# Column sums of ten conditioning halves: folded on VectorE and spread by one matmul, in a diffusion backbone layer on one core

## The chip, the core and the metric

The kernel runs on one NeuronCore of a Trainium2 chip. The metric is the time of one execution on the device, in microseconds (us), and the median of several runs stands for a kernel. The engines go by their short names: PE is TensorE (PEld its weight loads), DVE is VectorE, ACT is ScalarE, POOL is GpSimd, and SP issues most of the DMAs. Each engine runs its own list of instructions in order, and they meet only by semaphores.

## What is computed

One layer over 256 latent tokens (x) and 256 context tokens (y) of width 2048: a half-step SwiGLU block of width 5632, a mixer (gated recurrence and long convolution) behind one input projection, a second half-step SwiGLU block for the latent tokens, and a last norm. What matters for the change are the modulation vectors. Two vectors c are put through SiLU and multiplied by one large matrix; the nine parts of 2048 columns are shifts, scales and gates.

```python
mx = [m[:, None, :] for m in jnp.split(jax.nn.silu(c) @ ada_w[l] + ada_b[l], N_MOD, axis=-1)]
mc = jnp.split(jax.nn.silu(c_ctx) @ ada_w[l] + ada_b[l], N_MOD, axis=-1)

x = x + 0.5 * mx[2] * _swiglu(_modulate(_rmsnorm(x, norm_ffn1[l]), mx[0], mx[1]), ...)
y = y + 0.5 * mc[2] * _swiglu(_modulate(_rmsnorm(y, norm_ffn1[l]), mc[0], mc[1]), ...)
hc = _modulate(_rmsnorm(y, norm_mix[l]), mc[3], mc[4])
hx = _modulate(_rmsnorm(x, norm_mix[l]), mx[3], mx[4])
x = x + mx[5] * (mix_x @ w_out[l])
x = x + 0.5 * mx[8] * _swiglu(_modulate(_rmsnorm(x, norm_ffn2[l]), mx[6], mx[7]), ...)
return _rmsnorm(x, final_norm)
```

So parts 0 to 2 are needed in the first block, and parts 3 to 8 (mixer and second block) only after it. Of parts 5 to 8 only the latent vector counts.

## The kernel before

**Units.** All large weights stream in units of 128x1024 fp32 (512 KB). SP loads a unit into one of four raw buffers (`load_unit`), ACT rounds it to w_hi (L381), DVE takes the rest w_lo = raw - w_hi (L386), three units ahead of PE (`AHEAD`), and PE multiplies. In the first block each unit is 24 matmuls of 512 columns: for each of eight 128x128 blocks the three passes L396, L397 and L398. PE works through 24 units in each chunk of the first block: units 0 to 7 (j) are the up projections of the next chunk, 8 to 15 the down projection (`down`), and 16 to 23 again up. The down projection gives 16 output blocks d, two in each unit, and goes round three PSUM banks (4, 5, 6); when a block is done, DVE adds it to the residual stream in two instructions (`add`, L843), and only then may PE take that bank for block d + 3. Bank 7 is left for the modulation sums.

**Modulation.** The matrix has 18 halves of 1024 columns, each read in 16 tiles of 128 rows. Halves 0 to 3 are done in the prologue on PE. The rest are done by DVE beside the matmuls of the first block: `ada_step` multiplies a 128x1024 tile by a column of SiLU(c) and adds it to a running total (L610 for the first tile, L613 for the others). After 16 tiles the total, 128 lanes by 1024 columns, has to be summed over its lanes. `ada_total` (L640) does that on PE: for each 128x128 block of the total one fp32 matmul with a column of ones, which puts the sums of 128 columns along the lanes of bank 7. `ada_take` (L658, for halves 4 and 5 `ada_finish`) then copies them to `mods`.

**Order.** The chunks of the first block are `F1_LOOPS = ((1, 3), (4, 2), (4, 1), (1, 0))`: one chunk with halves 4 and 5 (ada 3), four iterations with one half for both vectors each (ada 2: halves 6 to 9), four iterations with two halves for the latent vector each (ada 1: halves 10 to 17), one chunk without, and then the last down projection. Where the steps and sums stand in the 24 units is written in `ada_steps`, `ADA_SUM_AT` and `ADA_TAKE_AT`: for ada 2 the 16 steps are in units 0 to 15, the sum behind unit 18; for ada 1 the steps are in units 0 to 7 and 11 to 18, the sums behind units 10 and 21. After the last down projection PE does the norm of the context (L455), DVE adds the bias to all the parts (`finish_mods`, L1867), and the mixer begins.

## Time and profile before

| | us |
|---|---|
| median of 3 runs | 3262.28 |
| lowest, highest | 3249.78, 3262.71 |
| the profiled execution's own time | 3266.25 |
| its span, from the first to the last instruction | 3264.5 |

The profile is of one execution. A group of instructions in it has a source line of the kernel, the engine, what it writes and reads, the count, the busy time, the mean ns of one, and the time for which the engine sat idle just before them with what ended it. PE's matmuls are pipelined, so one that is shown as 0.39 us long may start every 0.23 us: what a matmul costs in a row of them is read from the distance of the starts. An fp32 matmul is recorded as two. The granted clock (PEclk) is 1.00 at TensorE's upper level (2.4 GHz) and 0.50 at its lower one (1.2 GHz); a stretch in between holds a share of each.

### The profile page before, as it was taken

To read this page: it belongs to the slowest core of one execution; us is meant where nothing else is said; L and a number is where in the kernel's file an instruction comes from. 1 tells how busy PE (TensorE), PEld (TensorE's weight loads), DVE (VectorE), ACT (ScalarE), POOL (GpSimd) and SP (SyncE) were. 2 spreads that over 40 slices of the span, in tenths; PEclk is the share of its full clock that TensorE was granted. 3 is DMA by queue.
4 is the path that set the end of the run, shared out by engine and by line. 5 is a ranking of instruction groups with operands and counts; after the bars stand their busy time and mean duration, and the time that the engine had idled before them with its cause. 6 is when DMAs were issued, how large, how long until landed. Compare 5 with 4: busy or idle time off the path is not lost. (4 is left out here: it accounts for less than half of the span.)

```text
span 3264.5 us, 46521 instructions
## 1 busy us (share of the span) xinstructions
PE 3152.6 (97%) x17388; PEld 2694.0 (83%) x17388; DVE 2136.2 (65%) x2907; ACT 1262.5 (39%) x1687; POOL 187.9 (6%) x194
## 2 busy tenths in 40 slices
PE   6889999999999999999998999999998999999997
PEld 3348788888888888888877999999997888888886
DVE  5577747558475675756447767776666667766677
ACT  5452121222212222222236777753334444444443
POOL 3300000000000000000000023330000000000000
PEclk8889899999999999999999999999999999999998
DMA  8556545535446576665324554445545565666663
GB/s 299 181 193 185 176 147 150 180 129 173 146 143 219 187 238 214 223 218 173 97 91 123 162 175 149 148 142 187 163 145 152 184 190 182 185 190 184 186 185 110
DMA packets 438914, 563.25 MB, mean 173 GB/s; under 512 B 17856, under 2 KB 395065, under 8 KB 437897
## 3 DMA queue, kind: packets, MB, share of 16 engines
q1 hardware_dynamic: 432208, 545.80, 53.6%
q0 software_dynamic: 2816, 9.43, 0.9%
q10 hardware_dynamic: 3768, 6.37, 0.5%
q8 instruction: 81, 1.33, 0.2%
q14 instruction: 41, 0.33, 0.0%
HBM read 553.14 MB, written 8.39 MB: 172 GB/s over the span
## 5 line engine op out<-in xcount | busy, mean ns | idle before, releaser
L386 DVE TENSOR_TENSOR w_lo<-raw,w_hi 128x1024 fp32r<-128x1024 f32 x736 | 909.7, 1241 | 792.2 <-ACT w_hi L381 788.8
L381 ACT ACTIVATE w_hi<-raw 128x1024 fp32r<-128x1024 f32 x736 | 774.9, 1057 | 1365.6 <-PE bank L398 1067.1
L396 PE MATMUL bank<-h_hi,w_hi 128*128 128x512 f32 x1408 | 553.2, 393 | 0.2 <-DVE w_lo L386 0.2
L397 PE MATMUL bank<-h_lo,w_hi 128*128 128x512 f32 x1408 | 551.7, 392 | 0.0
L398 PE MATMUL bank<-h_hi,w_lo 128*128 128x512 f32 x1408 | 551.6, 392 | 0.0
L402 PE MATMUL bank<-h,w_hi 128*128 128x512 f32 x1408 | 500.9, 400 | 7.1 <-DVE h L473 6.6
L403 PE MATMUL bank<-h,w_lo 128*128 128x256 f32 x1408 | 396.6, 282 | 0.0
L613 DVE SCALAR_TENSOR_TENSOR states<-ada_raw,silu_c,states 128x1024 f32<-128x1024 f32 x300 | 375.9, 1281 | 2.3
L402 PEld LDWEIGHTS bank<-h,w_hi 128*128 128x128 f32 x1408 | 266.0, 189 | 74.5 <-DVE h L473 7.3
L396 PEld LDWEIGHTS bank<-h_hi,w_hi 128*128 128x128 f32 x1408 | 266.8, 189 | 56.5 <-issue 1.0
L398 PEld LDWEIGHTS bank<-h_hi,w_lo 128*128 128x128 f32 x1408 | 266.7, 189 | 56.3
L397 PEld LDWEIGHTS bank<-h_lo,w_hi 128*128 128x128 f32 x1408 | 266.8, 189 | 55.3
L396 PE MATMUL bank<-hx_hi,w_hi 128*128 128x256 f32 x1024 | 296.1, 289 | 0.0
L398 PE MATMUL bank<-hx_hi,w_lo 128*128 128x256 f32 x1024 | 289.6, 283 | 0.0
L397 PE MATMUL bank<-hx_lo,w_hi 128*128 128x256 f32 x1024 | 289.6, 283 | 0.0
L396 PE MATMUL bank<-g_hi,w_hi 128*128 128x512 f32 x704 | 277.9, 395 | 7.6 <-DVE y_res L843 4.8
L397 PE MATMUL bank<-g_lo,w_hi 128*128 128x512 f32 x704 | 276.9, 393 | 0.0
L398 PE MATMUL bank<-g_hi,w_lo 128*128 128x512 f32 x704 | 276.4, 393 | 0.0
L403 PEld LDWEIGHTS bank<-h,w_lo 128*128 128x128 f32 x1408 | 267.4, 190 | 0.0
L402 PE MATMUL bank<-g_both,w_hi 128*128 128x512 f32 x704 | 252.0, 402 | 6.2 <-DVE x_res L850 3.3
L403 PE MATMUL bank<-g_both,w_lo 128*128 128x256 f32 x704 | 198.8, 282 | 0.0
L397 PEld LDWEIGHTS bank<-hx_lo,w_hi 128*128 128x128 f32 x1024 | 196.3, 192 | 0.5 <-issue 0.2
(269 smaller groups left out, 4301.7 us busy)
## 6 DMA issues: line engine op xcount, KB each, us to landing
raw<-in_ffn_w_dram SPq DMA_DIRECT2D x528, 512.0 KB, 3.7
ada_raw<-in_ada_w_dram SPq DMA_DIRECT2D x256, 512.0 KB, 4.5
raw<-in_w_in_dram SPq DMA_DIRECT2D x176, 512.0 KB, 3.9
raw<-in_ada_w_dram SPq DMA_DIRECT2D x32, 512.0 KB, 4.5
raw<-in_w_out_dram SPq DMA_DIRECT2D x32, 512.0 KB, 3.6
spec<-spec_spill POOLq DMA_DIRECT2D x8, 768.0 KB, 5.0
spec_spill<-spec_out ACTq DMA_DIRECT2D x4, 1280.0 KB, 6.9
xin<-in_x_dram SPq DMA_DIRECT2D x1, 2048.0 KB, 14.1
```

Source lines behind the costliest of these rows:

```text
L381: nc.scalar.activation(w_hi[un.slot(j)][:], raw[un.slot(j)][:], ACT.Copy).then_inc(hi_done, 1)
L386: nc.vector.tensor_tensor(w_lo[un.slot(j)][:], raw[un.slot(j)][:], w_hi[un.slot(j)][:].bitcast(F32), ALU.subtract).then_inc(lo_done, 1)
L396: nc.tensor.matmul(o, w_hi[slot][:, c0:c0 + P], hi, start=start, stop=False, skip_group_check=True)
L397: nc.tensor.matmul(o, w_hi[slot][:, c0:c0 + P], lo, start=False, stop=False, skip_group_check=True)
L398: return nc.tensor.matmul(o, w_lo[slot][:, c0:c0 + P], hi, start=False, stop=stop, skip_group_check=True)
L402: nc.tensor.matmul(o, w_hi[slot][:, c0:c0 + P], both, start=start, stop=False, skip_group_check=True)
L403: return nc.tensor.matmul(o[:, 0:SEQ], w_lo[slot][:, c0:c0 + P], hi, start=False, stop=stop, skip_group_check=True)
L613: nc.vector.scalar_tensor_tensor(out=total, in0=src, scalar=silu_c[:, m, t:t + 1], in1=total, op0=ALU.mult, op1=ALU.add).then_inc(done, 1)
```

## The change

The two halves 4 and 5 stay as they are. For the other twelve halves, of which four are for two vectors (16 totals in all), `ada_total` on PE and `ada_take` go. In their place:

- DVE folds each total itself (`ada_fold_lanes`): 512 columns at a time it transposes 32x32 blocks from the total into bank 7, and sums each run of 32 along the row, which leaves 16 numbers on each lane. That is two transposes and two sums for each total. The numbers go to a 128x512 tile `ada_cols` that takes the place of the small `rows` tiles. The folds stand behind units 16 and 17 in the ada 2 iterations, and behind units 8 and 19 in the ada 1 iterations (`ADA_FOLD_AT`).
- Four partial sums are still apart, one in each group of 32 lanes. One fp32 matmul of 512 columns with a 128x128 matrix of zeros and ones, `same_lane`, adds them for all tiles at once (`ada_spread`). It stands ahead of unit 2 of the last down projection of the first block.
- Twelve copies of 32 lanes on DVE (`ada_gather`), behind unit 3 of the same down projection, bring the result into `mods`.
- `same_lane` is built by four small DVE instructions in the prologue (`lanes`), behind `bounds_rest` at tile 34. The 128x128 tile of ones shrinks to one column.
- The first step of a new total no longer waits for PE (L606), except in halves 4 and 5. PE gets a wait for the gathered values ahead of the norm L455.

```diff
-        ones_1 = sb("ones_1", [P, P])
-        rows = [sb(f"rows{n}", [P, P]) for n in range(4)]
+        same_lane = sb("same_lane", [P, P])
+        rows4 = sb("rows", [P, 4, P])
+        rows = [rows4[:, n, :] for n in range(4)]
+        ada_cols = rows4[:].rearrange("p n c -> p (n c)")
...
-        ADA_SUM_AT = {3: {2: (4, 0), 11: (3, 0)}, 2: {18: (2, 0)}, 1: {10: (1, 0), 21: (1, 1)}, 0: {}}
-        ADA_TAKE_AT = {2: {19: 0}, 1: {11: 0, 22: 1}}
+        ADA_SUM_AT = {3: {2: (4, 0), 11: (3, 0)}, 2: {}, 1: {}, 0: {}}
+        ADA_FOLD_AT = {3: {}, 2: {16: 0, 17: 1}, 1: {8: 0, 19: 1}, 0: {}}
...
-            if m == 0:
-                ve.wait_ge(ada_pe, ada_half(ada, it, n) + (0 if n else 1))
+            if m == 0 and ada >= 3:
+                ve.wait_ge(ada_pe, ada_half(ada, it, n) + 1)
...
-        def ada_take(ve, half, to, streams):
-
-            ve.wait_ge(ada_pe, half + 2)
-            nc.vector.tensor_copy(mods_flat[:, bass.ds(half * 8, 8), 0:streams],
-                                  bank[to][:, 0:16].rearrange("p (b t) -> p b t", t=2)[:, :, 0:streams]).then_inc(ada_out, 1)
+        def ada_fold_lanes(ve, ada, it, n):
+
+            total, done = ada_even[n], (ada_x, ada_c)[n if ada == 2 else 0]
+            nth = ada_folded(ada, it, n)
+            ve.wait_ge(done, ada_done(ada, it, 0 if ada == 2 else n, KB))
+            for h in range(2):
+                ve.wait_ge(ada_fold, nth + (2 * h + 1))
+                nc.vector.transpose(bank[7][:], total[:, h * 512:(h + 1) * 512]).then_inc(ada_fold, 1)
+                ve.wait_ge(ada_fold, nth + (2 * h + 2))
+                nc.vector.reduce_sum(ada_cols[:, bass.ds(nth * 8 + h * 16, 16)],
+                                     bank[7][:].rearrange("p (b i) -> p b i", i=32), mybir.AxisListType.X).then_inc(ada_fold, 1)
...
+        def ada_spread(pe):
+
+            pe.wait_ge(ada_fold, FOLDED)
+            pe.wait_ge(c_split, 6)
+            nc.tensor.matmul(bank[7][:], same_lane[:], ada_cols, start=True, stop=True).then_inc(ada_pe, 1)
+
+        def ada_gather(ve):
+
+            ve.wait_ge(ada_pe, 2 + 4 + 2)
+            for q in range(4):
+                lanes = slice(32 * q, 32 * q + 32)
+                src = bank[7][lanes, :].rearrange("p (i k q) -> p i k q", k=8, q=4)[:, :, :, q]
+                for t in range(2):
+                    nc.vector.tensor_copy(mods_flat[lanes, 6 * 8:10 * 8, t].rearrange("p (a k) -> p a k", k=8),
+                                          src[:, 0:8].rearrange("p (a t) k -> p a t k", t=2)[:, :, t])
+                ins = nc.vector.tensor_copy(mods_flat[lanes, 10 * 8:18 * 8, 0].rearrange("p (a k) -> p a k", k=8), src[:, 8:16])
+            ins.then_inc(ada_out, 1)
...
             for j in range(8):
+                if j == 2 and len(loops) > 1:
+                    ada_spread(pe)
                 down(un, j, j, N_CHUNK - 1)
...
-                    if ada in (1, 2) and j in ADA_TAKE_AT[ada]:
-                        ada_take(ve, ada_half(ada, it, ADA_TAKE_AT[ada][j]), 7, ada_streams(ada))
+                    if len(loops) > 1 and j in ADA_FOLD_AT[ada]:
+                        ada_fold_lanes(ve, ada, it, ADA_FOLD_AT[ada][j])
...
+                if j == 3 and len(loops) > 1:
+                    ada_gather(ve)
...
+            pe.wait_ge(ada_out, 8)
             norm_pe(pe, nctx, 512)
...
+            def lanes():
+                nc.vector.tensor_tensor(same_lane[:, 0:64], ident[:, 0:64], ident[:, 64:128], ALU.add).then_inc(c_split, 1)
+                ve.wait_ge(c_split, 3)
+                nc.vector.tensor_tensor(same_lane[:, 0:32], same_lane[:, 0:32], same_lane[:, 32:64], ALU.add).then_inc(c_split, 1)
+                ve.wait_ge(c_split, 4)
+                nc.vector.tensor_copy(same_lane[:, 32:64], same_lane[:, 0:32]).then_inc(c_split, 1)
+                ve.wait_ge(c_split, 5)
+                nc.vector.tensor_copy(same_lane[:, 64:128], same_lane[:, 0:64]).then_inc(c_split, 1)
```

What that does to the lists of instructions is seen at two places. The first is PE in the body of the ada 1 iterations, at the end of unit 10. Before, eight fp32 matmuls on blocks of the total (`states`) stand between the third pass of one unit and the first pass of the next:

```order
L396 MATMUL bank<-g_hi,w_hi 128x512
L397 MATMUL bank<-g_lo,w_hi 128x512
L398 MATMUL bank<-g_hi,w_lo 128x512
L707 ISA
L710 REGISTER_ALU
L640 MATMUL bank<-ones,states 128x1 x8
L690 REGISTER_ALU
L695 REGISTER_ALU
L396 MATMUL bank<-g_hi,w_hi 128x512
```

In the changed kernel nothing of this is in the loop bodies of ada 2 and ada 1, and the one matmul that takes its place stands in the last down projection (lines are those of the changed kernel):

```order
L401 MATMUL bank<-g_lo,w_hi 128x512
L402 MATMUL bank<-g_hi,w_lo 128x512
L681 MATMUL bank<-rows,same_lane 128x512
L400 MATMUL bank<-g_hi,w_hi 128x512
L401 MATMUL bank<-g_lo,w_hi 128x512
```

The second place is DVE in the same body, behind unit 8. Before, the next unit's w_lo follows the two residual additions at once:

```order
L843 SCALAR_TENSOR_TENSOR x_res<-bank,gate,x_res 128x256
L843 SCALAR_TENSOR_TENSOR y_res<-bank,gate,y_res 128x256
L386 TENSOR_TENSOR w_lo<-raw,w_hi 128x1024
L838 REGISTER_ALU
L843 SCALAR_TENSOR_TENSOR x_res<-bank,gate,x_res 128x256
```

In the changed kernel the four instructions of a fold stand between them:

```order
L879 SCALAR_TENSOR_TENSOR y_res<-bank,gate,y_res 128x256
L667 REGISTER_ALU
L669 ISA
L670 STREAM_TRANSPOSE bank<-states 128x512
L671 REGISTER_ALU
L672 ISA
L672 TENSOR_REDUCE rows<-bank 128x16
L669 REGISTER_ALU
L670 STREAM_TRANSPOSE bank<-states 128x512
L671 REGISTER_ALU
L672 ISA
L672 TENSOR_REDUCE rows<-bank 128x16
```

So both the w_lo of a later unit and the residual additions of unit 9 come behind the fold.

## Rows read from the trace of the kernel before

**Rows 1.** The page: busy time, then PE's granted clock in 40 slices.
```profile
PE 3152.6 (97%) x17388; PEld 2694.0 (83%) x17388; DVE 2136.2 (65%) x2907; ACT 1262.5 (39%) x1687; POOL 187.9 (6%) x194
...
PEclk8889899999999999999999999999999999999998
```

**Rows 2.** Groups by line, 560 to 1600 us (busy, mean ns, idle before).
```profile
L396 PE MATMUL bank<-h_hi,w_hi 128*128 128x512 f32 x1007 | 395.0, 392 | 0.0
```

**Rows 3.** Groups by line, whole span.
```profile
L640 PE MATMUL bank<-ones,states 128*128 128x1 f32 x320 | 38.0, 251 | 0.0
```

**Rows 4.** Timeline of PE (start, length) round a sum of 16 matmuls.
```profile
564.67 0.39 PE L398 MATMUL bank<-h_hi,w_lo 128*128 128x512 f32 x1
564.90 3.63 PE L640 MATMUL bank<-ones,states 128*128 128x1 f32 x32
568.38 0.49 PE L396 MATMUL bank<-h_hi,w_hi 128*128 128x512 f32 x1
568.71 0.40 PE L397 MATMUL bank<-h_lo,w_hi 128*128 128x512 f32 x1
```

**Rows 5.** The same round a sum of 8 matmuls.
```profile
1064.30 0.39 PE L398 MATMUL bank<-g_hi,w_lo 128*128 128x512 f32 x1
1064.53 1.84 PE L640 MATMUL bank<-ones,states 128*128 128x1 f32 x16
1066.23 0.49 PE L396 MATMUL bank<-g_hi,w_hi 128*128 128x512 f32 x1
```

**Rows 6.** Table of windows: busy time of each engine, then PEclk, DMA share, GB/s.
```profile
703.00:707.00 4.00, 4.00 (x12) 3.10 (x11) 0.07 (x1) 0.00 (x0) 0.00 (x0) 0.57 0.41 124
838.00:846.00 8.00, 8.00 (x31) 6.51 (x31) 0.17 (x1) 0.17 (x1) 0.00 (x0) 0.79 0.21 66
970.00:982.00 12.00, 12.00 (x56) 10.55 (x55) 1.40 (x2) 1.06 (x1) 0.00 (x0) 0.72 0.23 70
1050.00:1587.00 537.00, 537.00 (x2433) 446.79 (x2432) 326.66 (x377) 118.28 (x128) 0.00 (x0) 1.00 0.63 202
1675.00:1680.00 5.00, 4.75 (x14) 3.76 (x15) 1.43 (x3) 0.36 (x1) 0.00 (x0) 0.66 0.35 105
2510.00:3200.00 690.00, 690.00 (x3907) 598.35 (x3906) 489.74 (x732) 310.30 (x412) 0.00 (x0) 1.00 0.61 186
```

**Rows 7.** Groups by line, whole span: DVE instructions of 512 columns.
```profile
L805 DVE TENSOR_TENSOR xn<-xn,bank 128x512 f32<-128x512 f32 x22 | 14.1, 684 | 32.5 <-PE bank L398 32.5
...
L1979 DVE RECIPROCAL rstd<-root 128x512 f32<-128x512 f32 x4 | 13.4, 3342 | 0.0
```

**Rows 8.** Timeline of DVE: a copy of 512 columns.
```profile
1683.41 0.42 DVE L437 COPY sq_sum<-sq 128x512 f32<-128x512 f32 x1
```

**Rows 9.** Timeline of DVE behind units 8 and 19 of an ada 1 iteration.
```profile
1054.25 0.47 DVE L843 SCALAR_TENSOR_TENSOR y_res<-bank,gate,y_res 128x256 f32<-128x256 f32 x1
1054.94 1.23 DVE L386 TENSOR_TENSOR w_lo<-raw,w_hi 128x1024 fp32r<-128x1024 f32 x1 [0.22 <-ACT w_hi L381]
...
1062.01 0.48 DVE L843 SCALAR_TENSOR_TENSOR x_res<-bank,gate,x_res 128x256 f32<-128x256 f32 x1 [0.40 <-PE bank L398]
...
1117.68 1.23 DVE L386 TENSOR_TENSOR w_lo<-raw,w_hi 128x1024 fp32r<-128x1024 f32 x1 [5.27 <-ACT w_hi L381]
```

**Rows 10.** Timeline of DVE behind units 16 and 17 of an ada 2 iteration.
```profile
689.50 1.23 DVE L386 TENSOR_TENSOR w_lo<-raw,w_hi 128x1024 fp32r<-128x1024 f32 x1 [3.09 <-ACT w_hi L381]
694.94 1.23 DVE L386 TENSOR_TENSOR w_lo<-raw,w_hi 128x1024 fp32r<-128x1024 f32 x1 [4.21 <-ACT w_hi L381]
```

**Rows 11.** Timeline of PE: its one wait at a chunk's end, and the norm L455.
```profile
1675.25 0.50 PE L396 MATMUL bank<-g_hi,w_hi 128*128 128x512 f32 x1 [2.83 <-DVE g_lo L826]
...
1723.11 1.42 PE L455 MATMUL bank<-sq_sum,ones_d 128*128 128x512 f32 x2 [2.45 <-DVE sq_sum L440]
```

**Rows 12.** Timeline of DVE in the last down projection, behind unit 3.
```profile
1701.56 1.23 DVE L386 TENSOR_TENSOR w_lo<-raw,w_hi 128x1024 fp32r<-128x1024 f32 x1 [1.14 <-ACT w_hi L381]
```

**Rows 13.** Timeline of DVE in the prologue: the instruction that follows `bounds_rest`.
```profile
121.81 0.18 DVE L1789 RECIPROCAL hy_cols<-bank 128x4 f32<-128x4 f32 x1 [2.60 <-PE bank L1174]
```

More of the change, by code:

```diff
@@ L168, in build @@
         pairs4 = sb("pairs4", [P, 64])
+        one_col = pairs4[:, 2:3]
         lb = sb("lb", [P, 2, HEADS])
@@ L298, in build @@
         ada_x = sem("ada_x")
+        ada_fold = sem("ada_fold")
         ada_c = sem("ada_c")
@@ L640, in ada_total @@
                     ins = nc.tensor.matmul(bank[to][:, 2 * b + t:2 * b + t + 1], sums[t][:, b * P:(b + 1) * P],
-                                           ones_1[:, 0:1], start=fresh and b == 0 and t == 0, stop=True,
+                                           one_col, start=fresh and b == 0 and t == 0, stop=True,
                                            skip_group_check=True)
@@ L653, in ada_finish, with ada_folded @@
             ve.wait_ge(ada_out, nth + 2)
-        def ada_take(ve, half, to, streams):
-            ve.wait_ge(ada_pe, half + 2)
-            nc.vector.tensor_copy(mods_flat[:, bass.ds(half * 8, 8), 0:streams],
-                                  bank[to][:, 0:16].rearrange("p (b t) -> p b t", t=2)[:, :, 0:streams]).then_inc(ada_out, 1)
+        def ada_folded(ada, it, n):
+            return it * 8 + 4 * n if ada == 2 else it * 8 + (2 * ADA_BOTH * 4 + 4 * n)
+        def ada_fold_lanes(ve, ada, it, n):
[8 more added lines that the diff above has]
+                                     bank[7][:].rearrange("p (b i) -> p b i", i=32), mybir.AxisListType.X).then_inc(ada_fold, 1)
+        FOLDED = 4 * 4 * ADA_BOTH + 1
+        def ada_spread(pe):
[12 more added lines that the diff above has]
+            ins.then_inc(ada_out, 1)
         DOWN = {512: (4, 5, 6), 256: (4, 5, 6, 7)}
@@ L1014, in _ @@
             nc.gpsimd.memset(ones_h[:], 1.0 / DK).then_inc(memsets, 1)
-            nc.gpsimd.memset(ones_1[:], 1.0).then_inc(memsets, 1)
+            nc.gpsimd.memset(one_col, 1.0).then_inc(memsets, 1)
             for tile, r, n, src in ROWS:
@@ L1173, in l1_norm @@
                     for n in range(4):
-                        ins = nc.tensor.matmul(bank[4][:, blk:blk + 1], tabs[:, n // 2, n % 2, blk * P:(blk + 1) * P], ones_1[:, 0:1],
+                        ins = nc.tensor.matmul(bank[4][:, blk:blk + 1], tabs[:, n // 2, n % 2, blk * P:(blk + 1) * P], one_col,
                                                start=(n == 0 and blk == 0), stop=(n == 3), skip_group_check=True)
@@ L1707, in _ @@
             ve.sem_inc(ada_out, 1)
+            ve.sem_inc(ada_fold, 1)
             ve.sem_inc(xs["mix"], 1)
@@ L1821, in _ @@
                     bounds_rest()
+                    lanes()
                 if o in TAKE_AT:
@@ L1876, in _ @@
             ffn_dve(ve, fa, U_FFN1, g1, g1_hi, g1_lo, 512, [x_res, y_res], 0, F1_LOOPS, nctx, early_lo)
-            ve.wait_ge(ada_out, 1 + 2 * N_MOD)
+            ve.wait_ge(ada_out, 8)
             finish_mods(ADA_FIRST, N_MOD, 5)
```

## Prediction, made before the changed kernel was run

> **What bounds the kernel now.** The page comes first. PE is busy for 3152.6 of 3264.5 us and DVE for 65% [rows 1], so the first question is whether PE ever waits where the change works. The groups by line for 560 to 1600 us, which hold the eight loop iterations concerned but for the start of the first, answer it: the pass L396 has no idle time before it in 1007 matmuls, nor has the table of windows a moment in 1050 to 1587 us in which PE is not busy (537.00 of 537.00) [rows 2, 6]. ACT and DVE wait for PE there, and the weights are far ahead. In such a stretch each us that PE spends on something else lengthens the kernel by a us, and each us given back shortens it, as long as DVE keeps its dates. The sums over lanes, L640, are such work. They show no wait either [rows 3]; they stand in PE's row and cost what their issue takes.
>
> **What leaves PE.** Of the 320 records of L640, two for each fp32 matmul, 64 belong to halves 4 and 5 and stay. The other 256 are 128 matmuls: four sums of 16 (ada 2) and eight sums of 8 (ada 1). I take the price from the distance of starts, not from the busy time.
>
> - A sum of 16: the last regular matmul starts at 564.67, the next at 568.38, which is 3.71 us. Regular starts are 0.23 us apart, so the sum costs 3.48. The first start behind it takes 0.33 instead of 0.23, 0.10 more [rows 4]. 4 x 3.58 = 14.3 us.
> - A sum of 8: 1064.30 to 1066.23 is 1.93, less 0.23 is 1.70, and with the same 0.10 it is 1.80 [rows 5]. 8 x 1.80 = 14.4 us.
> - The clock. Behind the second, third and fourth sum of 16 the granted clock falls to 0.50, its lower level of 1.2 GHz, for a few us. A window of length W at mean clock c has lost W x (1 - c): 4 x 0.43 = 1.7, 8 x 0.21 = 1.7, 12 x 0.28 = 3.4, together 6.8 us [rows 6]. PE was in the row of one-column matmuls just before. Behind the eight sums of 8 the clock is 1.00 throughout, and so it is for 690 us of the second block, where nothing interrupts the wide matmuls [rows 6]. I take the three stretches to be due to the long sums.
>
> Together 14.3 + 14.4 + 6.8 = 35.5 us leave PE's row.
>
> The page "TensorE: Matmul & The Clock Gate" of the Trainium skill (What's actually happening) lets the clock fall after the array was idle. The rows do not agree in the letter: PE's records are busy for the whole of these windows. By the page's wording the stretches would have another cause and could stay; that is the second case below.
>
> **What PE gets.** One fp32 matmul of 512 columns. The same form is L455, 1.42 us from first start to modelled end, at the upper clock [rows 11]. Half of that is the least it can cost in a row of matmuls, all of it the most; I take 1.2, since the neighbours lose a little too. Its two waits are for folds made more than a chunk earlier and for the prologue. The new wait ahead of L455 is for copies that end more than 15 us before; PE waits there for DVE's squares anyway, 2.45 us [rows 11]. Nothing is added.
>
> **What DVE gets.** 16 folds of two transposes and two sums along rows. Neither form is in the trace. The nearest rows: an elementwise instruction of 512 columns that reads a bank, 0.684 us; below it a copy of 512 columns, 0.42; above it the reciprocal of 512, 3.342, the slowest of that width [rows 7, 8]. Between two DVE instructions that hang on a semaphore lies some 0.22 us (from 1054.72 to 1054.94) [rows 9]. So a fold F is 4 x (0.68 + 0.22) = 3.6 us, with 4 x 0.42 = 1.7 as the low end and 4 x 3.56 = 14.2 as the high end. I take 3.6, for one plain pass over 512 columns, as the additions are. The page "VectorE: DVE Perf Modes" of the Trainium skill speaks against the change here: among its rules for kernel authors `tensor_reduce` is called the slowest DVE operation, not to be put on a hot path, and its table of transposes has 311 ns for 128x128 bf16. Estimated from that page, four such widths for each transpose are 1.24 us and F is 4.7 us: the sum would be the same, as follows.
>
> What covers the folds:
>
> - Behind unit 8 (ada 1) is the tightest place. What queues behind the fold on DVE is a w_lo (1.23) and the addition of block 2 (some 0.9), and PE may not take that bank for block 5 before the latter is done. The fold starts at 1054.72; PE takes the bank as block 4 ends, just ahead of 1062.01 [rows 9]. 1061.9 - 1054.7 - 1.2 - 0.9 = 5.1 us of room. With F = 3.6 the additions of blocks 2 and 3 are late, by up to 2 us, and PE does not notice. The w_lo is for a unit three ahead, 3 x 5.45 us.
> - Behind unit 19 DVE idles for 5.27 us [rows 9]; behind units 16 and 17 (ada 2) it idles for 3.09 and 4.21 [rows 10]. The first is 0.5 us too short, which moves a w_lo that PE wants some 15 us later.
> - Later loads from SP follow w_lo and so move by as much; they have the same three units of room.
> - Twelve small copies behind unit 3 of the last down projection. Small copies of this kind start every 0.1 us or so; I take 1 to 2.5 us. DVE idles for 1.14 us in each unit there [rows 12], so it has caught up two units later, with four left. Without that cover: up to 2.5 us.
> - Four small instructions in the prologue, at most 1 us, where DVE then waits 2.60 us for PE [rows 13]. Without the cover: 1 us. The removed L658 copies and the wait at L606 give DVE back a little; nobody waits for it. POOL's smaller memset is worth nothing.
>
> **The sum.** -35.5 + 1.2 = -34.3 us. The profiled execution took 3266.25 us (span 3264.5, the rest outside), so 3232.0. The median of the runs is 4 us lower, at 3262.28; the same gain taken from it gives 3228. If that run had fewer half-clock stretches, which the changed kernel does not have at these places anyway, it would be 3232. I take 3230.
>
> **The rivals.**
>
> - *The half-clock stretches stay.* For: 1675 to 1680 us has one (0.66) with no long sum ahead [rows 6], and the rule above. Against: that one follows a wait of 2.83 us [rows 11], and the eight ada 1 sums and the second block have none. The gain is 27.5: 3235 to 3239.
> - *The fold is slower than its room, one form at the reciprocal's rate.* With the transposes at 3.34 us F is 2 x 3.56 + 2 x 0.90 = 8.9. PE waits 8.9 - 5.1 = 3.8 us in each ada 1 iteration, and behind a wait of that kind half clock costs 5 x 0.34 = 1.7 [rows 6, 11]. 4 x 5.5 = 22 us: 3252. It begins at F = 5.1. For: a transpose of fp32 is in no row. Against: only the reciprocal is so slow among DVE's forms.
> - *DVE becomes the bound, and the kernel is slower.* Both forms at that rate, F = 14.2: 4 x (9.1 + 1.7) = 43 us in ada 1. In ada 2 two folds take 28.4 us from 686.4, and with two w_lo (2.5) the w_lo of unit 21 is ready at 717; PE gets there at 710, some 15 us after that w_lo starts now [rows 10]: 4 x 7 = 28 us. 3230 + 71 = 3301. The point from which it costs more than PE gains is F of about 11 us. For: the page's warning. Against: nothing in the rows.
> - *The gain is there but does not show*, because runs differ by 13 us of themselves (3249.78 to 3262.71). Half the gain or less would be measured: 3247 to 3262.
>
> **How the numbers follow.** Forecast, 3222 to 3238: 0.65. Stretches stay, 3237: 0.15. Slow fold, 3252: 0.08. DVE the bound, 3301: 0.04. The gain not seen: 0.05. Something unnamed, slower: 0.03. The range should leave out no more than 0.2: it takes in the forecast's own range, the second case and the lucky runs on both sides, 3216 to 3248, and leaves out most of the last four. A measurement of this kernel can tell about 0.5% (16 us) from no change. Faster by more than that, below 3246: 0.65 + 0.15 and a little of the slow fold, 0.82. Within it: 0.11. Slower: 0.07.
>
> **What would show it.** L640 with 64 records instead of 320. An ada 1 iteration of 24 x 5.45 = 130.8 us, where units and two sums now make 134.4. No PE idle time in 560 to 1600 us, and PEclk 1.00 there. The four instructions of a fold at 0.5 to 0.9 us each. The addition of block 2 later than before. Wrong would be: PE waiting on DVE's additions in the ada 1 iterations (the fold was underpriced), matmul starts more than 0.23 us apart next to a fold (the two share something that I leave out), half clock in the ada 2 iterations without a sum, or a new wait at the last down projection.

## The result, and the profile after

The changed kernel took 3213.37 us (median of 4 executions, 3211.3 to 3214.48), the kernel before in the same comparison 3261.43 us (4 executions, 3249.78 to 3262.71). The ratio is 0.986 (95% interval 0.9836 to 0.9883): 46 us less by the ratio, where 34 had been forecast, and below the range of 3216 to 3248. A second comparison of the same two kernels, told below, gave 0.9897 (0.9873 to 0.992). Most of what follows asks which of the two is the change.

The profiled execution of the changed kernel took 3214.33 us (span 3212.5). Its page, the lines that answer to [rows 1]:

```profile
PE 3098.8 (96%) x17134; PEld 2654.9 (83%) x17134; DVE 2179.1 (68%) x2975; ACT 1262.2 (39%) x1687; POOL 187.6 (6%) x194
...
PEclk8889899999999999999999999999999999999999
```

PE is busy for 53.8 us less, DVE for 42.9 us more, and the span is 52.0 us shorter. What DVE got beside it, some 45 us of folds, did not show in the time.

The table of windows, of the eight loop iterations of the changed kernel (answers to [rows 6]; columns: busy time of PE, PEld, DVE, ACT, POOL, then PEclk, DMA share, GB/s):

```profile
549.00:1518.00 969.00, 969.00 (x4277) 802.37 (x4276) 657.43 (x754) 221.48 (x241) 0.00 (x0) 1.00 0.60 192
```

PE is busy in every moment of 969 us at the upper clock. The three half-clock stretches of [rows 6] behind the sums are gone, and no matmul waits. The fold behind unit 8 is what [rows 9] showed as two additions and a w_lo. Timeline of DVE in the changed kernel:

```profile
1033.48 0.48 DVE L879 SCALAR_TENSOR_TENSOR y_res<-bank,gate,y_res 128x256 f32<-128x256 f32 x1
1033.87 0.72 DVE L670 STREAM_TRANSPOSE bank<-states 128x512 f32<-128x512 f32 x1
1034.75 0.69 DVE L672 TENSOR_REDUCE rows<-bank 128x512 f32 x1 [0.17 <-DVE bank L670]
1035.48 0.73 DVE L670 STREAM_TRANSPOSE bank<-states 128x512 f32<-128x512 f32 x1
1036.35 0.69 DVE L672 TENSOR_REDUCE rows<-bank 128x512 f32 x1
1036.96 1.22 DVE L390 TENSOR_TENSOR w_lo<-raw,w_hi 128x1024 fp32r<-128x1024 f32 x1
1038.09 0.48 DVE L879 SCALAR_TENSOR_TENSOR x_res<-bank,gate,x_res 128x256 f32<-128x256 f32 x1
...
1038.88 0.48 DVE L879 SCALAR_TENSOR_TENSOR x_res<-bank,gate,x_res 128x256 f32<-128x256 f32 x1
...
1041.24 0.48 DVE L879 SCALAR_TENSOR_TENSOR x_res<-bank,gate,x_res 128x256 f32<-128x256 f32 x1 [0.36 <-PE bank L402]
```

From 1033.87 to the w_lo at 1036.96 are 3.1 us. The additions of blocks 2 and 3 (1038.09, 1038.88) follow one another without a wait, so they are late; the next one waits for PE again (0.36), so DVE has caught up. The spread matmul and its neighbours, timeline of PE:

```profile
1650.54 0.39 PE L402 MATMUL bank<-g_hi,w_lo 128*128 128x512 f32 x1
1650.76 1.02 PE L681 MATMUL bank<-rows,same_lane 128*128 128x512 f32 x2
...
1651.86 0.40 PE L401 MATMUL bank<-g_lo,w_hi 128*128 128x512 f32 x1
```

Regular starts are 0.227 us apart, so from 1650.54 to 1651.86, with one regular matmul between them, 0.454 would be due; the distance is 1.32, which makes 0.87 us for the spread.

Where the time went. The w_lo instructions of DVE are the same 768 in both kernels, so the distance between the same w_lo in both profiled executions shows where it changes:

| place | us less |
|---|---|
| prologue | -0.1 |
| four sums of 16, with the stretches behind them (3.63, 5.24, 5.23, 6.81) | 20.9 |
| eight sums of 8, 1.85 each | 14.8 |
| half clock at 1676 of before, absent after | 1.6 |
| spread matmul | -0.9 |
| start of the context part, where the half clock lies otherwise | -1.0 |
| one half-clock stretch in the mixer (2226 to 2232 of before), absent there after | 1.7 |
| just ahead of the second block | -0.5 |
| the second block, first to last matmul: 759.4 before, 744.8 after | 14.7 |
| behind the second block | 0.8 |

Together that is 52.0, the difference of the spans. Of the 36.5 us that are gained ahead of the second block, 34.8 are the sums and the spread. The prologue, with its four more instructions, loses 0.1 us; the other rows are places that the change doesn't touch. The row at 1676 is one of them: PE still waits 2.83 us there, as in [rows 11], only the half clock behind the wait is absent. Timeline of PE in the changed kernel:

```profile
1639.71 0.50 PE L400 MATMUL bank<-g_hi,w_hi 128*128 128x512 f32 x1 [2.83 <-DVE g_lo L862]
```

The biggest such row is the second block. The change touches no instruction of it. Still, the table of windows has PE busy and at the upper clock all the time in both, and more matmuls pass in 500 us. Before, then after:

```profile
2600.00:3100.00 500.00, 500.00 (x2831) 433.65 (x2831) 351.46 (x521) 223.25 (x298) 0.00 (x0) 1.00 0.61 186
```
```profile
2560.00:3060.00 500.00, 500.00 (x2887) 440.88 (x2886) 359.51 (x537) 227.30 (x302) 0.00 (x0) 1.00 0.61 189
```

There each pair is a matmul of 512 columns and one of 256 (below: wide and narrow). 2831 starts in 500 us are 0.353 us a pair, 2887 are 0.346. The block has 2112 pairs; times 0.007 that is 15 us. The row of starts shows how they differ. Timeline of PE, before:

```profile
2799.81 0.40 PE L402 MATMUL bank<-h,w_hi 128*128 128x512 f32 x1
2800.05 0.28 PE L403 MATMUL bank<-h,w_lo 128*128 128x256 f32 x1
2800.16 0.40 PE L402 MATMUL bank<-h,w_hi 128*128 128x512 f32 x1
2800.40 0.28 PE L403 MATMUL bank<-h,w_lo 128*128 128x256 f32 x1
2800.52 0.40 PE L402 MATMUL bank<-h,w_hi 128*128 128x512 f32 x1
```

And after:

```profile
2700.01 0.28 PE L407 MATMUL bank<-h,w_lo 128*128 128x256 f32 x1
2700.12 0.39 PE L406 MATMUL bank<-h,w_hi 128*128 128x512 f32 x1
2700.36 0.28 PE L407 MATMUL bank<-h,w_lo 128*128 128x256 f32 x1
2700.47 0.39 PE L406 MATMUL bank<-h,w_hi 128*128 128x512 f32 x1
```

Before, the distances wander between 0.233 and 0.241 behind a wide one and 0.113 and 0.120 behind a narrow one; after, they are 0.230 and 0.117 each time. I call 0.353 the long pitch of a pair and 0.347 the short one. A chip that is slower as a whole in one execution is not the reason: a unit of the first block takes 5.44 us in both.

### The profile page after: what moved, and what is told of

It reads as the page before. It is cut to its first block and busy times, and to the rows that moved or that the text cites. A ratio compares the mean times of both kernels' runs of the same rounds, so it can differ in the third digit from the quotient of the medians.

```text
span 3212.5 us, 46128 instructions
## 1 busy us (share of the span) xinstructions
PE 3098.8 (96%) x17134; PEld 2654.9 (83%) x17134; DVE 2179.1 (68%) x2975; ACT 1262.2 (39%) x1687; POOL 187.6 (6%) x194
## 5 line engine op out<-in xcount | busy, mean ns | idle before, releaser
L406 PE MATMUL bank<-h,w_hi 128*128 128x512 f32 x1408 | 491.1, 393 | 7.6 <-DVE h L477 6.6
L406 PE MATMUL bank<-g_both,w_hi 128*128 128x512 f32 x704 | 245.2, 392 | 7.8 <-DVE x_res L886 4.8
```

The source lines that it names most:

```text
L406: nc.tensor.matmul(o, w_hi[slot][:, c0:c0 + P], both, start=start, stop=False, skip_group_check=True)
```

## The experiments

Two things are tested: where the forecast's own terms come from (the long rows of one-column matmuls, the room behind unit 8, the folds), and whether the second block's 14.7 us belong to the change.

### Is the pitch a property of the kernel?

The kernel before, unchanged, in a new comparison.

> The kernel before, unchanged. In the profiled execution of it the two passes of the second block start 0.353 us apart in the pair, in that of the changed kernel 0.347, which is 14 us over the block's 2112 pairs; one of four runs of before was 12 us shorter than the others. Theory 1 (the pitch is settled anew each time the second block starts, by how its first matmuls fall against the clock's return to the upper level): the runs lie in two groups some 12 to 14 us apart, near 3262 and 3250, and the profile has one of the two pitches. Theory 2 (the program's own layout sets the pitch): all runs are near 3262 and the profile has 0.353.

Its 12 executions lie in two groups, 3246.8 to 3251.6 and 3259.5 to 3268.9, six in each; the ratio to the other executions of the same kernel is 1.0015 (0.9996 to 1.0034). Its profiled execution (3246.78 us) has the short pitch, window 2600 to 3100:

```profile
2600.00:3100.00 500.00, 500.00 (x2886) 440.87 (x2885) 362.67 (x543) 226.91 (x299) 0.00 (x0) 1.00 0.62 189
```

The second block took 746.0 us there and 759.4 in the profiled execution on which the prediction rests. So one and the same program has both pitches. Then one and three copies more on DVE just ahead of the second block, in the kernel before (the edit for three; for one, `range(1)`):

```diff
             rstd_dve(ve, n2, (0,))
+            for n in range(3):
+                nc.vector.tensor_copy(rows[n][:], ident[:])
```

> The kernel before with one copy of 128x128 on DVE (some 0.1 to 0.2 us) between the reciprocal and the scaling ahead of the second block, so that the block starts that much later. Theory 1: the pitch of the pair can come out at 0.353 or at 0.347, and the time near 3262 or 3249. Theory 2: 0.353 and 3262, since neither loops nor tiles move.

> The same with three copies (some 0.4 us). Theory 1: at least one of this and the run with one copy has the pitch 0.347 and a time near 3249. Theory 2: both have 0.353 and 3262.

One copy: 3250.18 us, ratio 0.9992 (0.9974 to 1.0011), short pitch in the profiled execution. Three copies: 3259.06 us, 1.0012 (0.9992 to 1.0031), long pitch. Both versions have executions near 3247 and near 3265, so the start of the block by the program does not fix the pitch. Two profiles alone would have looked like an effect of the copies; the timed executions say that it is none that can be told.

The changed kernel again:

> The changed kernel, unchanged, once more. Its four runs were 3211 to 3214 us and its profile had the short pitch (0.347 us for a pair of the second block). If the pitch is settled anew by each execution, its runs too lie in two groups, near 3213 and near 3226, and the ratio of means to before is about 3219 to 3254, 0.989: the change itself is worth 34 to 37 us, and the rest of the first result was the luck of the pitch. If the change itself brings the short pitch, all runs are near 3213.

3221.35 us (6 executions), ratio 0.9897 (0.9873 to 0.992), which is 33.5 us less than before (26 to 41). The ratio came as the first of the two cases had it, but its two clean groups did not: the executions took 3211.79, 3217.36, 3219.38, 3223.32, 3225.07 and 3226.98 us. The profiled execution took 3223.32 us, with the long pitch:

```profile
2560.00:3060.00 500.00, 500.00 (x2832) 433.54 (x2831) 351.72 (x523) 223.44 (x299) 0.00 (x0) 1.00 0.60 185
```

The second block took 758.1 us. Set beside the right partner, the change is seen without it: the block starts 36.5 us earlier in the first pair of profiled executions (2485.7 and 2449.2) and 34.9 earlier in the second (2479.6 and 2444.7), and from there on long is as long as long (759.4, 758.1) and short as short (746.0, 744.8).

The trace can be made to say it more sharply. Between two fixed w_lo, the one at 544.43 and the one at 1675.39 in the kernel before, lie all the sums and folds and nothing of the second block. The four profiled executions of kernels with rows of 16 (before, the same again, one copy, three copies) have 1130.96, 1129.35, 1130.99 and 1129.38 us there. The changed kernel has 1095.27 in both of its own, and in all its variants of this section but the one with longer folds. So what leaves PE there is worth 34.1 or 35.7 us, by the half-clock stretches that the execution before happened to have, and the spread takes 0.9 back.

What else differs between executions is seen in the same way. The w_lo at 544.43 comes between 539.3 and 545.0 in the fourteen profiled executions of this section, so the prologue alone scatters by some 5 us, in both kernels. That blurs the two groups. Of the 80 executions of the kernel before in the later comparisons 38 lie up to 3252.2, 29 from 3259.2 on and 13 in between.

### The long row of one-column matmuls and the clock

In the kernel before, the sum of 16 is cut into two of 8, behind units 16 and 20. The same 16 matmuls are issued.

```diff
-        ADA_SUM_AT = {... 2: {18: (2, 0)}, ...}
-        ADA_TAKE_AT = {2: {19: 0}, ...}
+        ADA_SUM_AT = {... 2: {16: (2, 0), 20: (2, 1)}, ...}
+        ADA_TAKE_AT = {2: {21: 0}, ...}
...
+                    if ada == 2 and n:
+                        ada_total(pe, ada_tiles(ada, 0), 7, (1,), False)
+                        return
```

> The kernel before with the four sums of 16 matmuls cut in two: 8 matmuls (the first vector) behind unit 16, 8 (the second) behind unit 20. Same work on PE. If the three half-clock stretches at the sums of 16 come from the long row of one-column matmuls: they vanish, PEclk is 1.00 from 560 to 990 us, and the first block ends 6.8 us less 0.4 (two more slow starts for each cut) earlier, some 6 us. If they have another cause they stay and the block is 0.4 us longer. The time then also depends on the second block's pitch: 3256 or 3243 with the first, 3263 or 3250 with the second.

3248.22 us, ratio 0.998 (0.996 to 0.9999), some 6.5 us less (0 to 13). In the profiled executions the four ada 2 iterations are 6.1 us shorter than before, where some 6 had been expected. The windows of [rows 6] in this kernel:

```profile
703.00:707.00 4.00, 4.00 (x22) 3.34 (x20) 1.22 (x1) 0.67 (x2) 0.00 (x0) 1.00 0.15 42
838.00:846.00 8.00, 8.00 (x44) 6.86 (x43) 2.42 (x3) 1.06 (x1) 0.00 (x0) 1.00 0.53 174
970.00:982.00 12.00, 12.00 (x62) 10.20 (x61) 2.54 (x3) 3.09 (x4) 0.00 (x0) 1.00 0.56 189
```

PEclk is 1.00 in all three, where it was 0.57, 0.79 and 0.72. Half-clock stretches follow 16 such matmuls in a row and not 8, with PE busy all along: the cause that the prediction took. Two rows of 16 stay in every kernel, those of halves 4 and 5, and fit: the first, at some 327 us, has a stretch at its end in all fourteen profiled executions, the second, at some 389 us, in nine. So such a row does not always bring one. The cut also moved the sums, from behind unit 18 to behind 16 and 20; that it is the length and not the place is borne out by these two rows, which stand behind units 2 and 11, and by the sums of 8 behind units 10 and 21 of ada 1, which have none.

The stretch at 1675 [rows 6] is absent in this kernel as well. It is another thing: it follows the wait of 2.83 us, which all fourteen profiled executions have, and it is there in eight of them, four of kernels with rows of 16, the last of these 700 us earlier, and four variants of the changed kernel. What decides whether it comes was not settled.

The ten executions are five from 3241.0 to 3242.4 and five from 3254.05 to 3254.5, nothing between: with most of the other scatter gone, the two pitches stand apart by 12.6 us.

### The folds, left out and made longer

Without the folds. The twelve halves' totals are then not summed over the lanes, so the modulation values of the mixer and of the second block are not computed.

```diff
-            for h in range(2):
-                ve.wait_ge(ada_fold, nth + (2 * h + 1))
-                nc.vector.transpose(bank[7][:], total[:, h * 512:(h + 1) * 512]).then_inc(ada_fold, 1)
-                ve.wait_ge(ada_fold, nth + (2 * h + 2))
-                nc.vector.reduce_sum(ada_cols[:, ...], bank[7][:].rearrange(...), ...).then_inc(ada_fold, 1)
+            nc.vector.tensor_copy(ada_cols[:, bass.ds(nth * 8, 32)], total[:, 0:32]).then_inc(ada_fold, 4)
```

> The changed kernel with the folds left out: one small copy of 32 columns stands for the two transposes and two sums of each total, so the modulation of the mixer and the second block isn't computed. PE's work is that of the changed kernel. If DVE hides the folds whole, nothing changes: the first block ends at the same time within 1 us (the last down projection begins at 1640 us), and the time is 3213 or 3226, by the pitch. If the folds cost PE something (banks given free later, matmuls slowed by DVE's use of bank 7), it is shorter by that, up to 5 us.

3221.11 us (3207.73 to 3227.6), ratio 0.9886 (0.9854 to 0.9918), beside 3221.35 with the folds. Its profiled execution has the same 1095.27 us between the two w_lo named above, and the long pitch in the second block. The folds, some 45 us of DVE, cost nothing.

Then a longer one: six more transposes of 512 columns ahead of the fold behind unit 8, in the four ada 1 iterations.

```diff
             ve.wait_ge(done, ada_done(ada, it, 0 if ada == 2 else n, KB))
+            if ada == 1 and n == 0:
+                for r in range(6):
+                    ve.wait_ge(ada_more, it * 6 + (r + 1))
+                    nc.vector.transpose(bank[7][:], total[:, 0:512]).then_inc(ada_more, 1)
+                ve.wait_ge(ada_more, it * 6 + 7)
...
```

> The changed kernel with six more transposes (0.72 us each, some 0.88 with the wait) ahead of the fold behind unit 8 of each ada 1 iteration, so that what stands there takes 3.1 + 5.2 = 8.3 us instead of 3.1. The results don't change. If the room behind unit 8 is 5.1 us, PE waits some 3.2 us for the residual addition of block 2 in each of the four iterations, and the granted clock falls for 3.4 us behind each wait (1.7 us more): 4 x 4.9 = 20 us, or 13 without the clock. If the room is greater (three units, as for the weights), nothing changes.

3244.76 us (10 executions), ratio 0.9962 (0.9944 to 0.998): 21 us above the same changed kernel by the ratios (0.9962 less 0.9897, of 3254). In its profile the four iterations lose 4.8, 2.9, 2.9 and 4.5 us. Timeline of DVE, then of PE, at the first:

```profile
1034.26 4.53 DVE L672 STREAM_TRANSPOSE bank<-states 128x512 f32<-128x512 f32 x6
...
1042.41 1.22 DVE L391 TENSOR_TENSOR w_lo<-raw,w_hi 128x1024 fp32r<-128x1024 f32 x1
1043.54 0.48 DVE L885 SCALAR_TENSOR_TENSOR x_res<-bank,gate,x_res 128x256 f32<-128x256 f32 x1
1043.93 0.48 DVE L885 SCALAR_TENSOR_TENSOR y_res<-bank,gate,y_res 128x256 f32<-128x256 f32 x1
```
```profile
1044.46 0.50 PE L401 MATMUL bank<-g_hi,w_hi 128*128 128x512 f32 x1 [2.88 <-DVE y_res L885]
```

PE now waits 2.88 us for the addition of block 2, the wait that the rival of the slow fold named. From 1034.26 to the w_lo at 1042.41 are 8.15 us; less 2.88 that leaves 5.3 us of room, where 5.1 had been worked out from [rows 9]. Two of the four waits (the 4.8 and the 4.5) are followed by a half-clock stretch, two are not. These four losses are 15.2 us, between the 13 and the 20 that had been expected; the remaining 6 of the 21 are within what the two intervals leave open.

The same trace has something that nobody put there. The second block begins with the short pitch and goes over to the long one at 2558 us, after 70 us of it, where a single matmul starts 0.05 us late. Its table of windows:

```profile
2500.00:2550.00 50.00, 50.00 (x290) 43.70 (x289) 31.83 (x45) 23.14 (x32) 0.00 (x0) 1.00 0.62 190
2570.00:2620.00 50.00, 50.00 (x285) 43.41 (x284) 32.02 (x46) 23.16 (x32) 0.00 (x0) 1.00 0.62 189
```

The granted clock is 1.00 throughout. So the pitch is not fixed for the whole block, even where nothing is inserted; the other nine profiled executions with an untouched block keep theirs to the end.

### Does the clock's return draw the pitch?

The block begins behind a pause of PE, at the lower clock. Eight matmuls with an unused result were put into this pause and the one ahead of the context part.

```diff
             norm_pe(pe, nctx, 512)
+            keep_busy(8)
...
             ins.then_inc(n2["mean"], 1)
+            keep_busy(8)
```

> The changed kernel with eight fp32 matmuls of 512 columns, written to a bank that nobody reads, behind the norm ahead of the context's projection and behind that ahead of the second block, where PE waits some 8 and 7 us for DVE. If the half clock with which both stages start comes from that pause, it is gone, both stages start at the upper level, and 4 us are saved (2.4 and 1.6). If moreover the long or short pitch of the second block is settled where the clock comes back while matmuls run, all runs now have one and the same pitch, and lie within 5 us of each other.

3222.57 us (3216.83, 3217.26, 3218.02 | 3227.12, 3228.27, 3232.38), ratio 0.9904 (0.9879 to 0.9929): no gain over 0.9897, and still two groups. The edit did only half of what it was for. The second block now begins at the upper clock, at 2445.80, but PE waits 2.55 us soon after, and the lower clock comes there instead, at 2460:

```profile
2448.00:2456.00 8.00, 8.00 (x48) 6.92 (x47) 6.70 (x15) 4.06 (x8) 0.00 (x0) 1.00 0.03 6
2460.00:2464.00 4.00, 3.78 (x13) 3.28 (x14) 3.48 (x4) 1.67 (x2) 0.00 (x0) 0.57 0.61 173
```

So the clock still comes back while the block's matmuls run, and this run by itself doesn't rule out that its return settles the pitch. What speaks against it is that the pitch also changes where the clock is 1.00 for long before and after: at 2558 us in the trace above, and in the next experiment.

### Interrupting the second block

Ahead of unit 16 in each of the ten loop iterations of the second block, one (then three) fp32 matmuls of one column, whose result is overwritten.

```diff
+                    if ntok == 256 and j == 16 and part == 0:
+                        for _ in range(1):
+                            nc.tensor.matmul(out(0)[:, 0:1], ones_d[:], sq_sum[:, 0:1], start=True, stop=True,
+                                             skip_group_check=True)
```

> The changed kernel with one fp32 matmul of one column (two records) ahead of unit 16 in each of the ten loop iterations of the second block; its result is overwritten. Priced at 0.11 us for a record and 0.10 behind it: some 0.3 us each, 3 us in all. Theory 1 (the pitch of the second block is drawn once, as the block begins or before): the trace shows one pitch of a pair, 0.347 or 0.353 us, from the first to the last iteration, and the timed executions fall into two groups some 13 us apart, about 3 us above the groups of the changed kernel (3215 and 3228). Theory 2 (it is drawn anew by every interruption of the regular row): the trace shows both pitches in turn, changing only at the inserted matmuls, and the timed executions gather within about 8 us around 3222. Rival: an interruption always ends in the same pitch; then all iterations after the first have it, in every execution, and the times are one group at 3216 or at 3228.

> The same with three such matmuls (six records) at each of the ten places: some 0.8 us each, 8 us in all. Theory 1 (drawn once): one pitch throughout the trace, two groups of times near 3220 and 3233. Theory 2 (drawn at every interruption): both pitches in one trace, changing at the inserted matmuls, one group of times around 3227. Rival (an interruption always ends in the same pitch): one pitch after the first iteration in every execution, 3220 or 3233.

One matmul: 3226.49 us (3222.36 to 3231.8), ratio 0.9915 (0.9893 to 0.9937). Three: 3230.54 us (3227.47 to 3232.25), 0.9925 (0.9903 to 0.9946). The table of windows of the kernel with one:

```profile
2620.00:2670.00 50.00, 50.00 (x285) 43.39 (x284) 33.12 (x49) 23.15 (x32) 0.00 (x0) 1.00 0.61 187
2685.00:2735.00 50.00, 50.00 (x290) 43.68 (x290) 32.29 (x47) 23.22 (x32) 0.00 (x0) 1.00 0.62 190
2750.00:2800.00 50.00, 50.00 (x285) 43.34 (x284) 30.98 (x43) 23.25 (x32) 0.00 (x0) 1.00 0.62 189
```

285 starts in 50 us is the long pitch, 290 the short one. It changes at an inserted matmul, holds to the next, and then changes back. The ten insertions cut the block into eleven pieces. With S for short and L for long they are, in this trace, LLL S LLL S LLL, and in that with three SLLL SLLL SLL, each with the clock at 1.00 at every insertion. So an interruption can change the pitch, and it is kept as long as the row is regular: Theory 1 and the rival, one pitch from some point on, are both out. But it isn't drawn by lot at each interruption either, as Theory 2 had it: every fourth piece is short in both traces. If five short pieces fell by chance among the 22, such an order would come in fewer than one case in a thousand. What the state is that these insertions move on by a step was not found.

The executions also come together, since each now has two or three short pieces of eleven in place of a block with one pitch: those with three inserted matmuls differ by 4.8 us, those of the changed kernel by 15.2. They lie some 4 us higher than expected (3226 and 3230 for 3222 and 3227), as more of the pieces are long than the even split behind these figures.

### Another order of wide and narrow

Last, the regular row itself: wide, wide, narrow, narrow in place of wide, narrow, wide, narrow, first in the up projections of the second block alone, then in the down projections too.

```diff
                 for b in range(2):
-                    last = two_pass(outs2[b], un.slot(j), k * 256 + b * P, hi(kb), both(kb), kb == 0, kb == KB - 1)
+                    nc.tensor.matmul(outs2[b], w_hi[un.slot(j)][...], both(kb), start=kb == 0, stop=False, ...)
+                for b in range(2):
+                    last = nc.tensor.matmul(outs2[b][:, 0:SEQ], w_lo[un.slot(j)][...], hi(kb), start=False, stop=kb == KB - 1, ...)
```

> The changed kernel with the order of the matmuls in the up projections of the second block changed from wide, narrow, wide, narrow (512 and 256 columns) to wide, wide, narrow, narrow; the down projections keep theirs. 704 groups of four, two thirds of the second block. Theory 1 (the two pitches belong to the alternation of wide and narrow, and a narrow matmul can follow a narrow one at 0.117 us): a group of four takes 0.69 us in every execution, the up projections are at the short pitch always, and the times lie at 3211 to 3218 us. Theory 2 (a narrow matmul of 0.117 us only keeps up because the load of its weights, 0.19 us long, lies beside the wide one ahead; behind a narrow one it has to wait): a group takes 0.05 to 0.07 us more, 35 to 50 us in all, and the times lie at 3250 to 3270.

> The changed kernel with wide, wide, narrow, narrow in the down projections of the second block too, not in the up projections alone. With the order in the up projections alone a group of four took 0.697 us in every part of the trace and the pairs of the down projections 0.353 (0.707 for four); the executions lay at 3218.6 to 3222.8. Theory 1 (the second pitch belongs to the alternation of one wide and one narrow): the 352 groups of the down projections also go to 0.697, which is 352 x 0.010 = 3.5 us less; a median of 3218 and a spread of 5 us or less. Theory 2 (the pitch is a matter of the down projections' operands or banks): they stay at 0.707, median 3222.

In the up projections alone: 3221.93 us (3218.59 to 3222.84), just above the 3211 to 3218 of Theory 1, ratio 0.99 (0.9874 to 0.9926). In both: 3216.66 us (3215.14 to 3219.19), 0.9895 (0.9879 to 0.9912). Timeline of PE of the latter (x2 merges two matmuls in a row), and its window:

```profile
2699.72 0.63 PE L415 MATMUL bank<-h,w_hi 128*128 128x512 f32 x2
2700.19 0.40 PE L418 MATMUL bank<-h,w_lo 128*128 128x256 f32 x2
2700.42 0.63 PE L415 MATMUL bank<-h,w_hi 128*128 128x512 f32 x2
2700.89 0.39 PE L418 MATMUL bank<-h,w_lo 128*128 128x256 f32 x2
```
```profile
2560.00:3060.00 500.00, 500.00 (x2873) 436.31 (x2872) 358.29 (x535) 226.28 (x302) 0.00 (x0) 1.00 0.61 188
```

A group of four starts every 0.70 us; by the count it is 0.696, or 0.348 a pair, near the short pitch. With the order in the up projections alone these have 0.697 for four in every part of the trace, while the pairs of the down projections keep 0.353. Once they are reordered they fall too. The second block took 751.5 and 748.1 us, against 744.8 (short) and 758.1 (long). So it is the alternation of single wide and single narrow matmuls that has the second pitch, as far as one trace of each order and ten executions without a 13 us split can show it. The rival, that a narrow matmul behind a narrow one has to wait for its weights, is out: its 35 to 50 us did not come.

Is the last version better than both kernels? It is faster than before by 34 us (29 to 39). Against the changed kernel the ratios (0.9895 and 0.9897) cannot be told apart, and its median lies above the 3213.37 of the first four executions. What it does is to narrow the scatter: 4 us between its four executions, 15 between the six of the changed kernel in its second comparison. Whether it lowers the mean would take more executions than there are here; the trace lets one expect 758.1 - 748.1 = 10 us when the changed kernel draws the long pitch, and a loss of 3 us when it draws the short one.

## Why the prediction was wrong

**What leaves PE: right.** 35.5 us were worked out, 35.7 is what the iterations show in the pair on which the forecast rests, and 34.1 with the execution before that had fewer half-clock stretches. A sum of 16 with no stretch gave 3.63 (3.58 forecast), a sum of 8 gave 1.85 (1.80). The clock's share, 6.8, is what is left of the other three sums of 16 (17.3 less 3 x 3.6 is 6.5), and cutting these sums in two brought 6.1 us in the trace. It was a little lucky in its size: in the other three profiled executions with rows of 16 the stretches lost 5.1, 6.8 and 5.1 us, always behind three of the four rows, not always the same three. The rival in which the stretches stay is out. The wording that it drew on, of the page "TensorE: Matmul & The Clock Gate" of the Trainium skill (What's actually happening), has the clock fall after an idle time; PE's records were busy for the whole of these windows here (4.00 of 4.00 us in the first [rows 6]), and the clock fell, so here the measurement decides.

**What PE gets: right.** 0.9 for 1.2.

**What DVE gets: right, and hidden.** 3.1 us for 3.6. Transposes of 512 columns took 0.723 and sums 0.692 in the mean of 32 each, so both ends of the range (0.42, 3.34) were far and the plain pass was the row to take. What made the fold shorter than forecast is the time between two instructions: 0.22 had been read from a wait for ACT [rows 9], and over the four it was 0.07 in the mean. The page "VectorE: DVE Perf Modes" of the Trainium skill (Rules for kernel authors) calls `tensor_reduce` the slowest DVE operation; here it took 0.692 us, and an elementwise addition of the same width 0.684 [rows 7], so for this form and width the measurement does not bear the warning out. The room of 5.1 us was right as well (5.3), so were the mechanism and the order of size of the rival that hung on it: by its working, F = 8.15 costs 3.05 us in each iteration and 1.7 more with a half-clock stretch; 2.9 was measured twice without one and 4.8 and 4.5 with one. It was wrong that such a stretch always follows: it did two times in four. The gather took 1.8 us, in the range of 1 to 2.5, and nobody waited.

**The step that failed is the last one, from the gain to the time and to the range.** The prediction took the gain from one profiled execution (3266.25 us) and noted that the runs differed by 13 us; it read that difference as small accidents of the clock at places that the change removes ("if that run had fewer half-clock stretches") and gave it 2 us. It also named the 13 us as noise that could hide the gain, but did not ask where in the program they arise. In fact most of them are the pitch of the second block, which has two values and differs from execution to execution (759.4 and 746.0 us for the block in two profiled executions of one program), and the profiled execution had the long one. In the later comparisons the kernel before ran 80 times, from 3242.75 to 3268.33 with a median of 3254.4, so the 3262.28 and 3266.25 from which the forecast was taken lie 8 and 12 us above its level. 3254.4 less 34.3 is 3220, and 7 us to each side for the pitch make 3213 and 3227: the ten executions of the changed kernel lie between 3211.3 and 3226.98. The range ended at 3216 and so left out the kernel's own short executions. The first four seem all to have been such, by their times (3211.3 to 3214.48); the one that was profiled was. With an even chance for each that happens once in sixteen times, and by its times the kernel before had three long ones of four beside them: the 46 us are in part luck. The hint stood in the times of before: 3249.78 beside 3262.28 and 3262.71 looks like two values rather than a spread.

With executions of like pitch compared, the forecast of 34.3 is met: 36.5 and 34.9 us by the start of the second block, 33.5 (26 to 41) by the second comparison of medians. The first comparison's 46 us hold some 12 that are no effect of the change.

**Left open.** What in PE decides which pitch a row falls into, the traces do not show, nor why every fourth piece was short. In ten profiled executions with an undisturbed alternating second block three had the short pitch to the end and a fourth for its first 70 us, while the timed executions of the kernel before split about evenly. Whether the chance differs between the kernels was not settled: only one execution of each comparison has a trace, and the ten of the changed kernel are too few.

## What to carry to other kernels

Where PE is busy without a gap, work of one column is priced by starts and not by columns: 0.11 us a record, two records for an fp32 matmul, and a long row of them can cost clock on top; such a sum over lanes moves to DVE at nothing but the one matmul that joins the four groups of lanes (0.9 us for all), if DVE has the room at each place, which is read off the first instruction behind it that somebody waits for. When a few timed executions already stand in two clusters, look for what differs between a profile from each before trusting any ratio, and compare like with like. The length of one stretch that the change does not touch, taken in both profiles, tells at once how much of a difference is luck, and the length of the stretch that it does touch tells what it is worth: here that was the same to 0.01 us in both profiled executions of the changed kernel, while its whole times differed by 15.

## What was not expected of the hardware

- A row that alternates matmuls of 512 and 256 columns at the upper clock has two stable pitches, 0.353 and 0.347 us a pair, with PE busy throughout. It kept one for the whole block, some 700 us, in nine of ten traces. It changed at inserted one-column matmuls, with every fourth piece short in both traces, and once, with nothing inserted, at a single start that came 0.05 us late. In the order wide, wide, narrow, narrow the one trace has 0.348.
- In each of four profiled executions the granted clock went to its lower level behind three of the four rows of 16 one-column fp32 matmuls between 560 and 985 us, with PE busy, at a loss of 1.7 or 3.4 us each time; behind rows of 8 it did so in none.
- A DVE transpose in blocks of 32 over 512 fp32 columns from SBUF to a bank takes 0.723 us, and the sum over runs of 32 in a bank 0.692.
